# Spreading the mLSTM stabiliser over the partitions with one-hot matmuls, and the mLSTM sums ordered head by head

## What is computed

```
h = RMSNorm(x)
q|k|v of attention, q|k, v, o, gates of mLSTM = h @ W_in     (3080 columns)
A = differential attention, 4 heads, causal, bucketed position bias
B = mLSTM (matrix memory with stabiliser m), 4 heads, by chunks
x = x + concat(A, B) @ W_out
x = x + MoE(RMSNorm(x))      (32 experts, top 4, 1024 wide)
out = RMSNorm(x)
```

```
num|den = (S * exp(a - m))^T-weighted sum of [v | 1]  +  (q * fade) @ state(t)
```

## Time and profile before

| what | value |
|---|---|
| median of 3 executions | 2267.07 us (2265.43 to 2267.86) |
| the profiled execution, its own time | 2265.43 us |
| its span in the trace | 2263.6 us |
| TensorE clock granted, mean | 0.988 of full speed |
| busy: PE, DVE, ACT, POOL | 97%, 62%, 25%, 11% |
| the chain that ended last: PE | 92% |

### The profile page before, as it was taken

How to read it: one execution, slowest core, us unless ns; L and a number is a source line. 1 busy time by engine, 2 the same in 40 slices (tenths; PEclk the granted TensorE clock), 3 DMA queues, 4 the chain that set the end, 5 groups by cost and what they waited for, 6 DMA issues and landing times.

```text
span 2263.6 us, 40201 instructions
## 1 busy us (share of the span) xinstructions
PE 2192.9 (97%) x14677; PEld 1893.8 (84%) x14679; DVE 1413.0 (62%) x2880; ACT 565.9 (25%) x1240; POOL 258.3 (11%) x235
## 2 busy tenths in 40 slices
PE   8999999999978999999999999999999999999996
PEld 4444554566668999999999999999999999999996
DVE  3352231678684777777778677764755566667567
ACT  2122221344311222222222222321221122222123
POOL 1000000121230110111001000110100000001013
PEclk9999999999988999999999999999999999999998
DMA  8000011210165899989989888976976788788688
GB/s 312 34 38 0 0 38 40 98 58 29 67 210 175 282 306 306 304 283 307 312 277 311 282 282 305 311 256 210 304 262 224 235 278 286 244 294 295 232 257 294
DMA packets 244662, 488.92 MB, mean 216 GB/s; under 512 B 24572, under 2 KB 24780, under 8 KB 244452
## 3 DMA queue, kind: packets, MB, share of 16 engines
q1 hardware_dynamic: 223684, 452.48, 57.3%
q0 software_dynamic: 20704, 35.60, 7.1%
q10 hardware_dynamic: 224, 0.16, 0.0%
HBM read 477.67 MB, written 49.63 MB: 233 GB/s over the span
## 4 chain that ended last, share of the span: by engine, by line
PE 92%; DVE 4%; issue 1%; ACT 1%; DMA 1%; POOL 0%; DVEq 0%; SPq 0%; POOLq 0%; ACTq 0%
PE PS L1024 66%; PE PS L664 15%; PE PS L851 5%; PE PS L791 1%; PE PS L824 1%; DVE pairA L1793 1%; PE PS L813 1%; PE PS L870 0%; DMA pairB<-acc_dram 0%; DVE unit L1522 0%; DVE pairA L1839 0%; PE PS L736 0%; DVE unit L1833 0%; PE PS L659 0%; PE PS L637 0%
## 5 line engine op out<-in xcount | busy, mean ns | idle before, releaser
L1024 PE MATMUL PS<-pairA,unit 128*128 x12288 | 1563.1, 290 | 31.3 <-DVE pairA L1839 11.9
L1024 PEld LDWEIGHTS PS<-pairA,unit 128*128 128x128 f32 x12288 | 1554.5, 191 | 40.0 <-issue 39.4
L1774 DVE STREAM_TRANSPOSE unit<-unit 32x512 f32<-32x512 f32 (+1 forms) x512 | 325.5, 636 | 10.3 <-DMA unit<-h_dram,cur_x 3.0
L1793 DVE STREAM_TRANSPOSE pairA<-unit 32x512 f32<-32x512 f32 (+1 forms) x512 | 325.8, 636 | 7.1
L664 PE MATMUL PS<-pairA,unit 128*128 128x512 f32 (+1 forms) x528 | 231.1, 594 | 1.4 <-issue 1.4
L1276 ACT ACTIVATE unit<-PS,cur_b 128x256 f32<-128x256 f32 x256 | 107.5, 471 | 414.9 <-PE PS L1024 414.9
L560 POOL DMA_INDIRECT unit<-h_dram,cur_x x66 | 68.8, 1042 | 1184.4 <-DVE cur_x L1829 1160.5
L664 PEld LDWEIGHTS PS<-pairA,unit 128*128 128x128 f32 (+1 forms) x528 | 97.4, 188 | 116.1 <-issue 115.4
L1259 ACT ACTIVATE unit<-unit 128x512 f32<-128x512 f32 x128 | 80.6, 630 | 453.8 <-DVE unit L1821 453.8
L1265 ACT ACTIVATE unit<-PS,cur_b 128x256 f32<-128x256 f32 x256 | 107.4, 471 | 317.7 <-PE PS L1024 314.2
L1813 DVE COPY cur_b<-b_all 128x24 f32 x32 | 6.7, 209 | 265.2 <-ACT unit L1276 261.3
(11 more groups left out here) (252 smaller groups left out, 1130.6 us busy)
## 6 DMA issues: line engine op xcount, KB each, us to landing
unit<-in_expert_w_gu_dram SPq DMA_DIRECT2D x256, 1024.0 KB, 5.1
unit<-in_expert_w_down_dram SPq DMA_DIRECT2D x128, 1024.0 KB, 8.2
unit<-in_w_in_dram SPq DMA_DIRECT2D x6, 2048.0 KB, 15.9
pairB<-in_x_dram SPq DMA_DIRECT2D x16, 512.0 KB, 5.9
unit<-in_w_out_dram SPq DMA_DIRECT2D x2, 2048.0 KB, 8.9
h_dram<-pairA SPq DMA_DIRECT2D x8, 512.0 KB, 2.6
acc_dram<-pairB SPq DMA_DIRECT2D x8, 512.0 KB
pairB<-acc_dram SPq DMA_DIRECT2D x8, 512.0 KB, 7.9
```

Source lines behind the costliest of these rows:

```text
L1024: ins = pe.matmul(ps[:, ITEM * (j % 2):ITEM * (j % 2) + w], slot_w[s][:, k, P * j:P * j + P], xa_cols[:, ITEM * kd:ITEM * kd + KD * ITEM + ...
L1774: ins = dve.transpose(cols[:, :, :, 32 * q:32 * q + 32], rows[:, :, :, 32 * a:32 * a + 32])
L1793: ins = dve.transpose(rows[:, :, :, 32 * a:32 * a + 32], cols[:, :, :, 32 * q:32 * q + 32])
```

## The change

The broadcast through HBM goes away: `wide_dram`, both DMAs and the semaphore `wide_out`. In its place PE multiplies a one-hot tile by `row_a`. POOL makes `pick`, a tile of 4 rows and 4 x 128 columns in which block h has ones in row h and zeros elsewhere; `pick[0:4, h, :]` as the stationary operand and 512 columns of `row_a` as the moving one give row h on all 128 partitions. There are 8 such matmuls (`widen`, 4 heads x 2 halves), two behind each of the MO outputs 0 to 3, in banks 6 and 7. ACT copies each into `m_wide` (`take_wide`). PE waits for these copies before it reuses a bank: inside `widen`, and before MO outputs 6 and 7.

In `ml_sums` the two loops over heads become one: for each head the 128-row product and, for t > 0, right behind it the 64-row product of the same head. Each head now opens its own accumulation.

Waits on `wide_ready` and `consts` get new counts. `pick` lies in the first 512 columns of `scratch`, which the mLSTM state takes later.

```diff
@@ sync
-            sp.wait_ge(em_in, 1)
-            sp.dma_start(wide_dram.rearrange("(h n) -> h n", h=MLH), row_a).then_inc(wide_out, 16)
-            sp.wait_ge(wide_out, 16)
-            sp.wait_ge(proj_done, after_group[MV])
-            sp.dma_start(unit[4][:, :], wide_dram.partition_broadcast(P)).then_inc(wide_ready, 16)
             sp.wait_ge(proj_done, after_group[K])
@@ gpsimd
             pool.memset(ones[:, :], 1.0).then_inc(consts, 1)
+            step.do(pool.memset(pick, 0.0))
+            pool.affine_select(out=pick, in_=pick, compare_op=ALU.not_equal, fill=1.0, base=0,
+                               pattern=[[-1, 4], [0, P]], channel_multiplier=1).then_inc(consts, 1)
@@ tensor, turn_gate_rows
-                pe.wait_ge(consts, 4)
+                pe.wait_ge(consts, 5)
@@ tensor
+            def widen(n):
+                if n >= 2:
+                    pe.wait_ge(wide_ready, n - 1)
+                pe.matmul(bank(6 + n % 2), pick[0:MLH, n // 2, :], row_a[:, HALF * (n % 2):HALF * (n % 2) + HALF],
+                          start=True, stop=True).then_inc(wide_ps, 1)
@@ tensor, ml_sums
                 for h in range(MLH):
-                    c = (DV + 1) * (h // 2)
+                    c, lo = (DV + 1) * (h // 2), 64 * (h % 2)
                     ins = pe.matmul(bank(2 + h % 2)[:, c:c + DV + 1], ml_w[:, t % 2, P * h:P * h + P],
-                                    ml_v[:, t, h, :], start=(h < 2), stop=(t == 0), skip_group_check=True)
-                for h in range(MLH if t else 0):
-                    c, lo = (DV + 1) * (h // 2), 64 * (h % 2)
-                    ins = pe.matmul(bank(2 + h % 2)[:, c:c + DV + 1],
-                                    ml_qs[lo:lo + 64, t % 2, P * (h // 2):P * (h // 2) + P],
-                                    ml_state[lo:lo + 64, t % 2, h // 2, :], start=False, stop=True,
-                                    skip_group_check=True)
+                                    ml_v[:, t, h, :], start=True, stop=(t == 0))
+                    if t:
+                        ins = pe.matmul(bank(2 + h % 2)[:, c:c + DV + 1],
+                                        ml_qs[lo:lo + 64, t % 2, P * (h // 2):P * (h // 2) + P],
+                                        ml_state[lo:lo + 64, t % 2, h // 2, :], start=False, stop=True)
@@ tensor, the MO outputs
             for n, o in enumerate(range(after_group[MV], after_group[MO])):
+                if n >= 6:
+                    pe.wait_ge(wide_ready, n + 1)
                 project(o)
                 if n == 0:
                     turn_gate_rows()
+                if n < 4:
+                    widen(2 * n)
+                    widen(2 * n + 1)
@@ scalar, take_out of K
                         act.wait_ge(cols_ready, 2)
+                        act.wait_ge(wide_ready, 8)
@@ scalar
+            def take_wide(n):
+                act.wait_ge(wide_ps, n + 1)
+                act.activation(m_wide[:, n // 2, HALF * (n % 2):HALF * (n % 2) + HALF], bank(6 + n % 2),
+                               ACT.Copy).then_inc(wide_ready, 1)
@@ scalar, the MO outputs
                 take_out(o)
                 if n < 4:
+                    take_wide(2 * n)
+                    take_wide(2 * n + 1)
                     act.wait_ge(conv_done, n + 1)
@@ scalar, ahead of the chunks
-            act.wait_ge(wide_ready, 16)
@@ vector, ahead of the chunks
-            dve.wait_ge(wide_ready, 16)
+            dve.wait_ge(wide_ready, 8)
...
-            dve.wait_ge(consts, 5)
+            dve.wait_ge(consts, 6)
```

More of the change, by code:

```diff
@@ L101, in build @@
     h2_dram = nc.dram_tensor("h2_dram", [SEQ, D + N_EXP], F32).ap()
-    wide_dram = nc.dram_tensor("wide_dram", [MLH * SEQ], F32).ap()
     acc_dram = nc.dram_tensor("acc_dram", [SEQ, D], F32).ap()
@@ L158, in build @@
         above = scratch[:, 896:1024]
+        pick = kn(scratch[:, 0:512], 4)
         lam_in = kn(scratch[:, 512:768], 4)
@@ L294, in build @@
             "x1_squared", "x1_mean", "x1_rstd", "logits_read", "g_all_ready"))
-        out_sent, wide_out = sem("out_sent"), sem("wide_out")
+        out_sent = sem("out_sent")
         spot_ready, last_summed = sem("spot_ready"), sem("last_summed")
```

## The result

The changed kernel takes 2286.92 us (median of 6, 2284.26 to 2297.29) against 2265.62 us (median of 6, 2261.25 to 2267.86) for the kernel before: ratio 1.0098, 95% interval 1.0085 to 1.011. It is slower by 21.3 us; 2286 had been forecast. All but one of the 25 runs of the changed kernel on record lie between 2283.76 and 2290.54 us. The profiled execution took 2288.99 us, span 2287.2 us, against 2265.43 and 2263.6.

What follows compares the result with a forecast made beforehand. PE, busy for 97% of the span, was taken to bound the kernel: 8.0 + 11.2 = +19.2 us on 2265.43 gives 2284.6, forecast as a median of runs at 2286 us; range 2276 to 2292 us.

Steps and rivals of the forecast that it cites:

- The transfer is worth nothing: Broadcast of `m_wide`: the tile lies ready 25 us before its first reader, so removing the two DMAs gains nothing.
- Part 1: Eight `widen` matmuls on PE: 16 records of 0.429 us plus changes of shape, +8.0 us, bounds 6.9 to 8.4.
- Part 2: `ml_sums` head by head: a step takes 3.33 us against 1.73, seven steps, +11.2 us.
- the partner is the neighbouring matmul: `ml_sums`: a 64-row record runs in twos with the neighbouring matmul on the other half of the rows; 0.11 us a slot.
- The upper bound: `ml_sums`: each of 8 changes a step waits until the record before has ended, 3.9 us more, 15.1 us.
- The estimate that the prediction made from its pages: `ml_sums`, with the skill's 166 ns: 6 more changes and 4 lost pairs, 1.4 us a step, about 10 us in all.
- Part 3: Work beside PE (ACT's eight copies, DVE, POOL's memset and select): hidden, 0 us, up to 0.5 if room is tight.
- the loose end of the clock: Wait in the DA stage: a half-clock stretch, seen at 400 us, costs up to 3.4 us and can come or go.
- Free changes of shape: Rival, 12%: changes of shape nearly free between small groups; +7 to +11 us, 2274 to 2278.
- Waiting for the accumulated region: Rival, 14%: every change waits for the accumulated region, or one more half-clock stretch in DA stage; +21 to +27 us.
- A delay eaten later: Rival, 3%: PE's idle time between 645 and 680 us absorbs 16.3 of the 19.2 us; +2.9 us, 2270.
- A transfer that held something: Rival, 1%: the 2 MB beside PE, or an earlier first mLSTM step, gives back 20 us or more.

Runs made afterwards that it cites:

- late4: Kernel before with the broadcast issued four MO outputs later; 0.00 us from gate transposes to DA logits, 2261.38 us whole (one run) against 2260.54.
- late7: Kernel before with the broadcast issued seven MO outputs later; +4.38 us from gate transposes to DA logits, 2264.36 us whole (one run) against 2260.54.
- widen_only: Changed kernel with the old order of `ml_sums`; against the kernel before, +8.14 us from gate transposes to DA logits, ratio 1.0049.
- sums_only: Kernel before with the head-by-head order of `ml_sums`, broadcast kept; +11.23 us from gate transposes to DA logits, ratio 1.0054.
- sums_halves: Kernel before with the 64-row products of `ml_sums` in head order 0, 2, 1, 3; +0.05 us from gate transposes to DA logits, 2261.79 us whole (one run).
- sums_twos: Kernel before with `ml_sums` by twos: two 128-row products, their two 64-row ones, then the other heads; +2.76 us from gate transposes to DA logits, ratio 1.0008.
- joined: Kernel before with the scores of chunk t + 1 right behind `ml_sums(t)`, t = 1 to 6; -2.36 us from gate transposes to DA logits, ratio 0.9988.
- after_third: Changed kernel run a third time, unchanged; against the kernel before, +19.38 us from gate transposes to DA logits, 2283.76 us whole (one run).
- turn_more: Kernel before with the 16 transposes of 4 rows done four times over; +4.61 us from gate transposes to DA logits, 2252.46 us whole (one run).

## Why the prediction was right

**The transfer is worth nothing.** Right, and with more room than I read: the tile lay ready for 25 us before its first reader, but DVE and ACT had room behind it too, 47 us in all (`late4`, `late7`).

**Part 1, 8.0 us.** Measured 8.14 (`widen_only`). The rows say 4 x 0.429 for each pair whatever the number of rows; a pair takes 1.91 with its way in and 7.06 - 6.87 = 0.19 on the way out, 2.10 against 2.11 forecast; the first 1.82 against 1.72; why behind the transposes 0.10 us is lost even so, no run shows.

**Part 2, 11.2 us.** Measured 11.23 (`sums_only`). The size came out right from L791, a short 64-row group of the trace. That the partner is the neighbouring matmul was wrong (`sums_halves`). It did no harm here by luck: a lone Q leaves the other half idle by either reading, so both give the same sum. The upper bound, a wait until W's record has ended, didn't come: each change of shape costs the same 0.2 us though Q adds onto what W has just written.

The rule of the Trainium skill on the change of tiling mode (TensorEngine Tiling (Array Packing), Key Properties) agrees with these runs as far as they go: each change costs 0.2 us, in `sums_twos` and `joined` too, and a change of half inside a 64-row group costs nothing (0.65 us in `sums_halves`). Whether the 0.2 us are a drain, no run shows. The estimate that the prediction made from its pages, 10 us, was low by 1.2.

**Part 3, 0 us.** Right: POOL's memset and select took 0.52 and 0.64 us, and POOL still idled 1.74 us before its first `rstd`:

```profile
1.98 0.52 POOL L473 MEMSET scratch<- 128x512 f32 x1
2.64 0.64 POOL L474 TENSOR_SCALAR_AFFINE_SELECT scratch<-scratch 128x512 f32<-128x512 f32 x1
...
5.66 0.57 POOL L484 TENSOR_TENSOR rstd<-ssq,neg_half 128x1 f32<-128x1 f32 x1 [1.74 <-DVE ssq L1329]
```

**The sum.** 19.2 us were forecast; a profile of the changed kernel without the half clock near 150 us shows 19.38 over the stage (`after_third`). What the profiled execution has beyond, 23.6 of span, is that stretch (1.7), and the rest, 2.5, behind the stage. The prediction lacked both. It looked for the loose end of the clock only at 400 us and did not ask what the new matmuls themselves do to it; and it let the later stages only shift. From the first DA logits to the first matmul of the experts' loop the kernel before takes 288.58 us and the changed one 291.75; the five profiles with `widen` have 290.5 to 291.8, eight of the nine without it 288.5 to 289.9, and the ninth, `turn_more`, 290.8. What makes this 1 to 3 us was not looked for.

That 2286 came within a microsecond of 2286.92 is in part luck: 21.3 us were measured and not 19.2, and the kernel before, over six runs, has a median 1.45 us below the one that the forecast started from.

**The rivals.** Free changes of shape: refuted by `sums_twos`. Waiting for the accumulated region: refuted by the 0.42 us groups. Its other half, one more stretch at half clock in the DA stage: a stretch came, but near 150 us and in two of three profiles; from 395 to 440 us the clock is 0.89 and not 0.92, which `late4` and `sums_halves` show too. A delay eaten later: the loss of the stage, 21.06 us, arrives whole at the end. A transfer that held something: refuted by `late4`.

## What to carry to other kernels

On a path that is PE alone, a DMA with 47 us of room is free and a matmul that replaces it is not: here f32 matmuls of 4 rows by 512 columns cost what those of 128 rows cost, 0.43 us a record. Keep matmuls of one shape together: every change between 128-row and 64-row products cost 0.2 us here, nearly two records of 129 columns, and 64-row products ran at double rate only while both halves of the rows had work in the same group. A short group that stands alone in the trace of before (here L791, 0.42 us) can price such an order before it is tried.

## What was not expected of the hardware

PE's clock fell to 1.2 GHz with PE never idle, during or just behind work on 4 rows: in 2 of 4 profiles with 2.9 us of it in one piece, and in the one with 4.0.

`turn_more` did 64 transposes where 16 do, lost 4.61 us by the first DA logits, and yet took 2252.46 us, 6.5 below the lowest of all 37 runs of the kernel before (2259.01). It wins this in the experts' first item. PE's timeline there, first of the kernel before, then of `turn_more`, with the idle time before each group:

```profile
652.47 18.12 PE L1024 MATMUL PS<-pairA,unit 128*128 x128 [7.59 <-issue]
679.41 18.29 PE L1024 MATMUL PS<-pairA,unit 128*128 x128 [8.82 <-DVE pairA L1839]
705.31 18.98 PE L1024 MATMUL PS<-pairA,unit 128*128 x128 [7.60 <-DVE pairA L1782]
```

```profile
659.42 17.89 PE L1025 MATMUL PS<-pairA,unit 128*128 x128 [9.16 <-issue]
678.13 16.37 PE L1025 MATMUL PS<-pairA,unit 128*128 x128 [0.81 <-issue]
694.70 32.69 PE L1025 MATMUL PS<-pairA,unit 128*128 x256 [0.20 <-issue]
```

There PE waits 0.8 and 0.2 us where the kernel before waits 8.8 and 7.6, and its clock is granted 0.96 of full speed from 640 to 760 us, not 0.89. From the first of these matmuls to the 513th, the kernel before takes 88.95 us (652.47 to 741.42) and `turn_more` 68.55 (659.42 to 727.97); the other twelve profiles take 82.1 to 88.8. The whole of what lies behind the first DA logits takes 1893.4 to 1902.3 us in those thirteen and 1882.0 in `turn_more`, so much of the scatter of whole executions arises in this item. Whether `turn_more` brings its gain about or met it by chance, one run can't say, and why it happens is open.
